# First channel tile's base beside the last projection tiles, and a new memory layout for the branches' stage

## What is computed

```
z = h @ in_w                                  # stage P: 92 tiles of 128 channels
r, k, v = mix(z_rkv, shift(z_rkv), mu)        # branch A: token shift on a 4-row grid, then a mix
kk = l2_normalize(k * k_k)                    # per head of 64
decay, a = lora(...)                          # per direction
y_A = sum over directions of the chunked RWKV recurrence (chunks of 128 tokens)
q, k, v = silu(conv3(z_qkv)); k, q = l2_normalize(k), l2_normalize(q)
y_B = sum over directions of the chunked gated delta rule (chunks of 128 tokens)
y = concat(groupnorm(y_A) ..., rmsnorm(y_B) ...)
```

## Time and profile before

| | us |
|---|---|
| median of 3 runs | 4016.66 (4015.81 to 4019.03) |
| profiled execution | 4017.41 |
| its span in the profile | 4015.6 |
| TensorE busy (matmul) | 3739.2 (93%) |
| VectorE, ACT, POOL busy | 2098.3 (52%), 1504.2 (37%), 1654.0 (41%) |
| stage P | 1300 to 2047 |
| stage B | 2047 to 3054 |
| stages C and M | 3063 to 4015 |

### The profile page before, as it was taken

The page is one execution under the profiler, slowest core; times in us unless marked ns, Lnnn a source line. Parts: engine busy times, 40 slices in busy tenths (PEclk is TensorE's granted clock), DMA queues, the critical chain, the costliest instruction groups (busy, mean ns, idle before and its releaser), DMA issues. The chain is left out here.

```text
span 4015.6 us, 86008 instructions
## 1 busy us (share of the span) xinstructions
PE 3739.2 (93%) x37240; PEld 3456.6 (86%) x37240; DVE 2098.3 (52%) x3807; ACT 1504.2 (37%) x2641; POOL 1654.0 (41%) x1192
## 2 busy tenths in 40 slices
PE   6998999898899899999979999999998999999998
PEld 5888888788888788888868888888887999999998
DVE  4434433533443677666766666666655653434343
ACT  3333343333343443232223333333333444444343
POOL 4444455444454454333321111111113656666664
PEclk9999999899999999999979999999998999999999
DMA  4344444344444576767720000001004545555553
GB/s 186 142 173 153 162 173 169 134 158 158 145 158 160 174 273 245 276 245 267 284 76 27 27 19 14 23 27 27 7 2 170 190 177 183 184 181 183 184 187 128
DMA packets 115672, 587.21 MB, mean 146 GB/s; under 512 B 20832, under 2 KB 40160, under 8 KB 50528
## 3 DMA queue, kind: packets, MB, share of 16 engines
q1 hardware_dynamic: 115296, 581.71, 40.8%
HBM read 560.95 MB, written 20.71 MB: 145 GB/s over the span
## 5 line engine op out<-in xcount | busy, mean ns | idle before, releaser
L543 PE MATMUL bank<-act_L,part_L 128*128 128x256 f32 x7296 | 972.2, 292 | 5.7 <-POOL act_L L3020 4.0
L543 PEld LDWEIGHTS bank<-act_L,part_L 128*128 128x128 f32 x7296 | 923.8, 197 | 46.4 <-issue 25.9
L2980 POOL TENSOR_TENSOR part_L<-wring,part_L 128x512 fp32r<-128x512 f32 x304 | 528.4, 1739 | 631.9 <-ACT part_L L1311 631.8
L543 PE MATMUL bank<-act_P,part_P 128*128 128x512 f32 (+1 forms) x3488 | 716.9, 365 | 18.1 <-POOL part_P L2980 12.7
L2980 POOL TENSOR_TENSOR part_C<-wring,part_C 128x512 fp32r<-128x512 f32 x320 | 568.7, 1786 | 369.9 <-ACT part_C L1311 369.9
L543 PEld LDWEIGHTS bank<-act_P,part_P 128*128 128x128 f32 x3488 | 591.3, 189 | 137.6 <-DVE arena_P L2408 16.2
L543 PE MATMUL bank<-arena_B 64*64 64x64 f32 (+4 forms) x13472 | 567.1, 227 | 28.7 <-DVE arena_B L2485 19.0
L543 PEld LDWEIGHTS bank<-arena_B 64*64 64x64 f32 (+3 forms) x13472 | 512.5, 141 | 70.2 <-DVE arena_B L2485 22.3
L2022 DVE TENSOR_TENSOR part_L<-wring,part_L 128x512 fp32r<-128x512 f32 x304 | 228.9, 754 | 524.8 <-ACT part_L L1311 524.8
L2980 POOL TENSOR_TENSOR part_P<-wring,part_P 128x512 fp32r<-128x512 f32 x184 | 307.0, 1674 | 432.0 <-ACT part_P L1311 432.0
L543 PE MATMUL bank<-act_Y,part_C 128*128 128x258 f32 (+1 forms) x3840 | 464.7, 283 | 9.3 <-POOL part_C L2980 9.3
(11 more groups left out here) (248 smaller groups left out, 3459.4 us busy)
## 6 DMA issues: line engine op xcount, KB each, us to landing
wring<-in_w SPq DMA_DIRECT2D x404, 1024.0 KB, 4.8
arena_P<-in_w SPq DMA_DIRECT2D x64, 1024.0 KB, 5.0
mring<-in_w SPq DMA_DIRECT2D x32, 1024.0 KB, 5.7
z_kept<-arena_P SPq DMA_DIRECT2D x34, 256.0 KB, 5.6
z_kept<-arena_P SPq DMA_DIRECT2D x58, 128.0 KB, 5.9
xT<-z_kept SPq DMA_DIRECT2D x26, 256.0 KB, 2.7
arena_C<-z_kept SPq DMA_DIRECT2D x32, 128.0 KB, 2.8
cst<-z_kept SPq DMA_DIRECT2D x24, 128.0 KB, 2.1
```

Source lines behind the costliest of these rows:

```text
L543: return e.matmul(out, lhsT, rhs, start=start, stop=stop)
L2980: e.tensor_tensor(wl[:, 4:8, :], wring[s % NS][:, 8 * j + 4:8 * j + 8, :], wh[:, 4:8, :].bitcast(F32), sub).then_inc(*mark("pool_lo", "lop ...
```

## The change

Three things are done together.

1. The memory of stage B gets names. The arena is cut into seven parts by what stage P has in them: `parts` (weights), `h` (activations, with `yr` in it), `made` (norm buffers, free after tile 16), `mid` (modulation), `stores` (the four buffers `B.zst`) and `top` (not used by stage P). What tile 0's base writes goes into `made` and `top`; what only the tails and the second direction's end use (`R.pr`, `R.bon`, `R.tp`, `R.s`, `R.bv`, `R.gate`, `g.Y`) goes into `stores`. So the wait of ACT, VectorE and POOL for the last four stores at the start of stage B is gone; VectorE waits for them just ahead of `R.pr` in the preparation of direction 0.
2. `base_a(0)` is taken out of stage B and runs in stage P's `early`, after tile 84; the loop `base_a` in stage B begins at tile 1. The word `("base", 0)` has then been said when stage B begins. `FIRST_B`, `PAD` and the `LATE` constants stay. The load of tile 0's LoRA weights moves to SP's `early`, behind `load_b(0)`.
3. The clearing for direction 0 is shared out anew: VectorE clears `NA` and `AK` ahead of everything in stage B (`rzv`), POOL clears `RK`, `RB`, `XT` right after direction 0's copies of the identity, and direction 1's copies move behind branch B's.

```diff
@@ -378,18 +378,23 @@
-            pools = [arena_(37088), xT_] + wring_ + [cst[:, o:o + 1920], par[:, PAR["wa2"][0]:PAR["wa2"][0] + 512]]
-            used = [0] * len(pools)
-
-            def alloc(n, order=(0, 1, 2, 3, 4, 5, 6)):
+            whole_B = arena_(37088)
+            pools = {"xT": xT_, "cst": cst[:, o:o + 1920], "wa2": par[:, PAR["wa2"][0]:PAR["wa2"][0] + 512]}
+            pools.update((f"w{i}", x) for i, x in enumerate(wring_))
+
+            pools.update((name, whole_B[:, a:b]) for name, a, b in (
+                ("parts", 0, 8192), ("yr", 8192, 12288), ("h", 12288, 24576), ("made", 24576, 26880), ("mid", 26880, 32000),
+                ("stores", 32000, 34048), ("top", 34048, 37088)))
+            used = dict.fromkeys(pools, 0)
+
+            def alloc(n, order=("parts", "h", "mid", "w0", "w1", "w2", "xT", "cst", "wa2", "top", "made", "stores")):
                 for i in order:
-                    whole = pools[i]
-                    if used[i] + n <= whole.shape[1] - (4096 if i == 0 else 0):
+                    if used[i] + n <= pools[i].shape[1]:
                         used[i] += n
-                        return whole[:, used[i] - n:used[i]]
+                        return pools[i][:, used[i] - n:used[i]]
                 raise MemoryError(n)
-            B.yr = pools[0][:, 37088 - 4096:].rearrange("p (k t) -> p k t", k=16)
-            early = (1, 5, 6)
+            B.yr = pools["yr"].rearrange("p (k t) -> p k t", k=16)
+            early = ("xT", "cst", "wa2")
@@ -400,6 +405,12 @@
+            R.kT, R.vT, R.kkn, R.z = [alloc(512, ("made",)) for _ in range(4)]
+            R.rT = alloc(256, ("made",))
+            lo_ = alloc(768, ("top",))
+            R.Vt = [alloc(512, order) for order in (("top",), ("parts",))]
+            R.rrk = alloc(256, ("top",))
+            R.pr, R.bon, R.tp, R.s, R.bv, R.gate = [alloc(256, ("stores",)) for _ in range(6)]
@@ -410,10 +421,9 @@
-            lo_ = alloc(768)
             R.lo = lo_.rearrange("p (j c) -> p j c", j=6)
-            R.kT, R.vT, R.z, R.a, R.cc, R.e1, R.e2, R.kkn = [alloc(512) for _ in range(8)]
-            R.Vt = [alloc(512).rearrange("p (q c) -> p q c", q=4) for _ in range(2)]
+            R.a, R.cc, R.e1, R.e2 = [alloc(512) for _ in range(4)]
+            R.Vt = [x.rearrange("p (q c) -> p q c", q=4) for x in R.Vt]
@@ -429,9 +439,8 @@
-            R.rT, R.rrk, R.pr, R.bon, R.tp, R.s, R.bv, R.gate = [alloc(256) for _ in range(8)]
             for g in R.d:
-                g.Y, g.Rd = alloc(256), alloc(256)
+                g.Y, g.Rd = alloc(256, ("stores",)), alloc(256)
@@ -937,6 +969,8 @@
+                yield from weave.until(("ptile", 84))
+                yield from base_a_tile(0)
@@ -1922,8 +1940,6 @@
-            for n in range(NPR - 4, NPR):
-                w.wait_ge(done("zs", n))
@@ -2409,6 +2425,40 @@
+
+            def base_a_tile(c):
+                V = "dve_rwkv"
+                yield
+                for key, dst, n in (("r", R.rT, c), ("k", R.kT, 8 + c)):
+                    w.wait_ge(done("z", key, c))
+                    w.wait_ge(done("part", key, c))
+                    stt(dst, D.S[key], P("mu", n, 1), dst, mult, add).then_inc(*mark(V, "mixed", key, c))
+                yield
+                w.wait_ge(done("z", "v", c))
+                w.wait_ge(done("part", "v", c))
+                w.wait_ge(done("mixed", "k", c))
+                ts(R.kkn, R.kT, P("kk", c, 1), None, mult, None).then_inc(*mark(V, "kk0", c))
+                ts(R.rrk, R.rT, P("rk", c, 1), None, mult, None).then_inc(*mark(V))
+                stt(R.vT, D.S["v"], P("mu", 16 + c, 1), R.vT, mult, add).then_inc(*mark(V, "mixed", "v", c))
+                yield
+                BS.take()
+                b, u = BS.take()
+                w.wait_ge(done("sums", ("kk", c)))
+                ts(small(2), b[:, 0:8], 1.0, 1e-12, mult, add).then_inc(*mark(V, "free", "bs", u))
+                counts.at[("mean", ("kk", c))] = counts.last(V)
+                yield
+                b, u = BS.take()
+                w.wait_ge(done("spread", ("kk", c)))
+                tt(R.kkn, R.kkn, b, mult).then_inc(*mark(V, "free", "bs", u))
+                counts.at[("zfree", c, 0)] = counts.last(V)
+                yield
+                weave.said.add(("base", c))
+
+            def base_a():
+                for c in range(1, 8):
+                    yield from weave.until(("prep", c - 1, 1))
+                    yield from weave.rest(LATE_A)
+                    yield from base_a_tile(c)
@@ -2547,6 +2599,8 @@
+                    for n in range(NPR - 4, NPR):
+                        w.wait_ge(done("zs", n))
@@ -2578,6 +2632,7 @@
+                    w.wait_ge(done("rzv"))
@@ -2622,41 +2677,6 @@
-            def base_a():
-                V = "dve_rwkv"
-                for c in range(8):
-                    if c:
-                        yield from weave.until(("prep", c - 1, 1))
-                        yield from weave.rest(LATE_A)
...
-                    if c == 0:
-                        for x in (R.d[0].NA, R.d[0].AK, R.d[0].RK, R.d[0].RB, R.d[0].XT):
-                            e.memset(x, 0.0).then_inc(*mark(V, "rz", 0))
...
@@ -2849,8 +2869,8 @@
-            for n in range(NPR - 4, NPR):
-                w.wait_ge(done("zs", n))
+            for x in (R.d[0].NA, R.d[0].AK):
+                e.memset(x, 0.0).then_inc(*mark("dve_rwkv", "rzv"))
@@ -3069,9 +3089,15 @@
+            def early():
+                yield from weave.until(("ptile", 84))
+                yield from base_a_tile(0)
+
             def tail(stage, n0, n1):
                 for n in range(n0, n1):
                     yield from project(stage, n)
+                    if stage == "P":
+                        weave.said.add(("ptile", n))
@@ -3203,18 +3231,19 @@
-            weave.run(tail("P", 0, NPR), behind=behind)
+            weave.run(tail("P", 0, NPR), early(), behind=behind)
             weave.run(behind)
             ends("pool", "P")
             begins(w, "P")
-            for n in range(NPR - 4, NPR):
-                w.wait_ge(done("zs", n))
-            for d in range(2):
-                for Q in R.d[d].Q:
-                    e.tensor_copy(Q.rearrange("p (u s) -> p u s", u=8), bc(C("id64"), 8)).then_inc(*mark("pool_rwkv", "qid", d))
+            for Q in R.d[0].Q:
+                e.tensor_copy(Q.rearrange("p (u s) -> p u s", u=8), bc(C("id64"), 8)).then_inc(*mark("pool_rwkv", "qid", 0))
+            for x in (R.d[0].RK, R.d[0].RB, R.d[0].XT):
+                e.memset(x, 0.0).then_inc(*mark("pool_rwkv", "rz", 0))
             for d in range(2):
                 for Q in G.d[d].Q:
                     e.tensor_copy(Q.rearrange("p (u s) -> p u s", u=4), bc(C("id64"), 4)).then_inc(*mark("pool_gdn", "gqid", d))
+            for Q in R.d[1].Q:
+                e.tensor_copy(Q.rearrange("p (u s) -> p u s", u=8), bc(C("id64"), 8)).then_inc(*mark("pool_rwkv", "qid", 1))
@@ -3368,6 +3397,7 @@
+                e.dma_start(lo_, LORA[0]).then_inc(*mark("dma_lora", "lora", 0))
@@ -3379,8 +3409,8 @@
-                w.wait_ge(done("gate", i - 1) if i else done("w0h"))
-                e.dma_start(lo_, LORA[i]).then_inc(*mark("dma_lora", "lora", i))
+                    w.wait_ge(done("gate", i - 1))
+                    e.dma_start(lo_, LORA[i]).then_inc(*mark("dma_lora", "lora", i))
```

More of the change, by code:

```diff
@@ L3087, in gpsimd, with base_a_tile, base_a @@
             ends("pool", "L")
+            def base_a_tile(c):
+                for _ in range(3):
+                    yield
+                root(("kk", c), small(2), 8)
+                yield
+                yield
+                weave.said.add(("base", c))
+            def base_a():
+                for c in range(1, 8):
+                    yield from weave.until(("prep", c - 1, 1))
+                    yield from weave.rest(LATE_A)
+                    yield from base_a_tile(c)
             def inverse(tag, XP, XT, Q, n, sem):
@@ L3123, in thread_a @@
                     weave.said.add(("chain", c, d))
-            def base_a():
-                for c in range(8):
-                    if c:
-                        yield from weave.until(("prep", c - 1, 1))
-                        yield from weave.rest(LATE_A)
-                    for _ in range(3):
-                        yield
-                    root(("kk", c), small(2), 8)
-                    yield
-                    yield
-                    weave.said.add(("base", c))
             def tail_a():
```

120 lines of the change are left out of this document (49 added, 71 removed).

## The result

The changed kernel takes 4077.53 us (median of 5 runs, 4074.4 to 4086.23) against 4019.03 us for the kernel before beside it (5 runs, 4015.81 to 4022.39): ratio 1.0148, 95% interval 1.0133 to 1.0163. The forecast was 4055.7 us in a range of 4004 to 4080, with 0.69 on slower. Side and mechanism hold; the size is 22 us short, more than a third of the loss. The profiled execution of the kernel after took 4086.23 us; it is the slowest of the five, 8.7 us above their median, and its mean granted clock is 0.961 where the other four have 0.963. So sizes read from it are some 9 us larger than the median's, and by that difference of 0.002 over 4080 us about 8 of the 9 belong to the clock (an estimate).

What follows compares the result with a forecast made beforehand. TensorE (93% busy) was taken to decide on the average, but what counts is whether VectorE is loaded in the same steps. 4017.4 - 6 (start) + 45 (phase) = 4056.4, less 0.75: 4055.7 us, range 4004 to 4080.

Steps and rivals of the forecast that it cites:

- The seam (part 1): Seam between projections and branches: direction 0 starts 13.8 - 2.7 = 11.1 us earlier, its transposes at 2063.0.
- The start (part 2): First period of stage B: the earlier start is worth 6 us, between 2 and 14.
- The phase (part 3): Stage B's periods: A six steps ahead of B makes VectorE's bursts meet, +6.4 us seven times, 45 us.
- The steps named: Sign in stage B: TensorE waits for VectorE where B's convolutions (L2764/L2766/L2772) stand beside A's preparation (L2561 to L2565).
- The other pair that was named: Sign in stage B: TensorE also waits for VectorE where L2716 stands beside L2547; no separate size.
- a step lasts as long as the longer of the two: Stage B: each step takes the longer of TensorE's and VectorE's work; 121.0 us a period before, 127.8 after.
- Rival (c): Stage B: low clock behind 14 new waits, 14 x 3 = 42 us more, 4098; chance 0.06 above 4080.
- one in three: Stage B: only one in three of the 14 new waits brings the low clock, 4070, inside the range.
- Rival (a): Stage B: phase costs nothing, bursts slip into VectorE's 38% free; 4010.7 us, from 4003 to 4015; chance 0.22.
- (b): Both halved: start -6, phase +1 to +2 us a period, seven times; 4018 to 4025; chance 0.10.
- (d): Seam: TensorE stalls beside the projection for the root, start gives 3 instead of 6 us; no chance of its own.
- The end of the stage: End of stage B: A finishes six steps earlier, B's last chain runs alone; 0 to +2 us, taken as 0.

Runs made afterwards that it cites:

- e4: Kernel after with FIRST_B = 5 instead of 10, branch A one step further ahead of B than in the kernel before: 4029.10 us, ratio 1.0030.
- e1: Kernel after with FIRST_B = 4 instead of 10, so both branches stand to each other as in the kernel before: 4006.92 us, ratio 0.9975.
- e3: Kernel after with tile 0's base put back behind the seam, keeping the new memory layout and moved loads: 4016.99 us, ratio 1.0000.
- e6: Kernel before without two of the three taps of each convolution of branch B: 4013.40 us, ratio 0.9989.
- e2: Kernel before with FIRST_B = 16 instead of 10, putting branch A six steps ahead of B: 4086.97 us, ratio 1.0174.
- e5: Kernel after without two of the three taps of each convolution of branch B: 4038.89 us, ratio 1.0051.
- e11: Kernel after with branch B's tanh of k on ScalarE issued one step later, behind branch A's copies: 4090.52 us, ratio 1.0180.
- e7: Kernel after with FIRST_B = 7 instead of 10, branch A three steps further ahead of B than in the kernel before: 4078.52 us, ratio 1.0151.
- e10: Kernel before with LATE_B = 7 instead of 3, branch B's base pieces four steps later: 4066.74 us, ratio 1.0123.
- e12: e1 with branch B's tanh of k on ScalarE issued one step later: 4008.37 us, ratio 0.9978.

## Why the prediction was right, and where it was short

**The seam (part 1)** held in its times: lw at "about 2051" came at 2051.09 and at full clock, the transposes expected at 2063.0 came at 2063.91, and the last projection matmul ended 2.3 us later, near the 2.7 priced for TensorE's added work. One pair of traces can't confirm that price, though: in the traces of kernels that are the same up to there, this matmul ends anywhere from 2048.11 (e4) to 2053.36 (e1) with the base beside the projection, and from 2046.83 (e3) to 2049.28 (e6) without. One of its grounds was wrong: the wait for the last stores, named first among what is removed, had held nothing up by itself, since e3, which removes it without moving the base, is at 1.0000.

**The start (part 2)** is the first wrong step. It was to be worth 6 us at the point where branch A's step 28 and branch B's step 22 end, at 2120 against 2126. They end at 2126.51: worth nothing. Its first stretch is right (put at 2080, measured 2078.76). The second, twelve steps, was priced at 27.9 us of work, 6.5 for the low clock and 6 of waiting, 40 us; it took 47.75, of which 9.9 are waiting and, with the 27.9 of work taken as they were priced, 9.9 the clock (10.3 by the low stretches of the trace). So the hole was not closed but moved: from the seam to this point TensorE is idle for 27.2 us, after 28.3 before. Up to the transposes the waits shrink from 18.78 us (7.36 + 3.22 + 8.20) to 12.54 (1.67 + 10.87), but behind them 14.6 follow, as I read it since branch A runs alone there at first and TensorE has nothing of branch B to put between. With branch B brought back beside it (e1), the stage is 10.4 us shorter than before: the start is worth more than the 6 us, but only with the phase kept.

**The phase (part 3)** is right in its mechanism. The steps named (L2764 and L2766 beside L2561 to L2565) are where the 3.2 us wait stands; e1 and e2 show that the shift is the cause, e5 and e6 that more than half of it is the convolutions on VectorE meeting branch A's preparation, and e11 that ScalarE's order in between is not. The rest, by the waits, is branch B's chain updates behind the same preparation. The other pair that was named, L2716 beside L2547, ends none of TensorE's waits in stage B of the kernel after. The periods were to be 126 to 128 us. Counted from lw of direction 1 in one tile to that in the next, the seven are 125.9 to 133.1, 129.3 in the mean, against 120.1 before. The term was put at +6.4 us a period and is +9.2 in the profiled run, and it is two terms: +4.2 of waiting (idle time of 6.9 us a period before, 11.0 after), which the sum over-priced by half, and 4.9 of clock (2.4 before, 7.3 after), which had no place in it; in the median run the clock's part is about 1 us smaller. So the step that failed is "a step lasts as long as the longer of the two": it is a rule for waits, somewhat high for them, and blind to what comes behind them. That the measured time still lies in the range, 2.5 us under its top, is partly luck: the waits were priced some 15 us too high and the clock's 28 to 37 us were left out, beside the 6 of the start.

**Rival (c)** had the missing term, and its price was right for the wrong number: 14 waits of 2 to 3 us at 3 us each, 42 us; measured are 37 us for the clock, on top of 30 instead of 45 us of waiting. Nor were there 14 waits of that size but seven, of 2.8 to 3.2 us; of the other new ones between 2130 and 2970 us none is over 1.4. It was given "one in three" inside the range and 0.06 above it. The trace of before had the warning, a window at 0.50 behind a wait of 1.18 us and 80 us of low clock in the stage; a change that adds waits of nearly three times that length in seven places must be priced with the clock in the sum, not beside it. The Trainium skill (TensorE: Matmul & The Clock Gate, "HAM oscillation") tells of waits that come again and again, there for DMA, and bring the clock down each time. The trace agrees in that the low clock came at each of the seven longest waits and fills 161 us of stage B instead of 80; how long it lasts is not the same each time here, 3.4 to 13.7 us.

**Rival (a)**, that the phase costs nothing because VectorE has 38% of its time free, is refuted. VectorE is busy only 491 of 840 us in the kernel after (526 before, when more of the work fell into them), and is nevertheless what the added time hangs on. The Trainium skill (Perfetto Trace Analysis, "Identifying the Most-Contended Engine") has the engine with the highest occupancy optimized first, for TensorE judged rather by its weight loads than by its matmuls. That is TensorE by either (85% and 92%). The trace does not bear that order out here: VectorE's 3.96 us a period weigh 38.6 us in one order of the steps and 4.0 in the other. (b) and (d) did not come about.

The end of the stage was taken at 0 to +2 us; stage C's first matmul was put at about 3100 and came at 3133.70, late by the missing term and the start, and nothing behind it changed.

## What to carry to other kernels

Where two streams are interleaved in fixed steps, add up each step's work per engine before anything is started earlier: a start that moves one stream against the other changes every later period, and seven periods outweigh any seam. The cure is then to move the other stream by the same amount (here FIRST_B = 4 instead of 10, which turns +58.5 us into -10.7). And when waits of a microsecond or more are added to a stream of matmuls, price the lower clock behind them at about as much as the waits themselves, in the sum and not beside it; that is the middle of a wide spread (see below), so the range must take it in too.

## What was not expected of the hardware

- A wait can cost more through the clock than by itself. Per us of added idle time, the clock took 1.2 us in the kernel after (37.0 for 30.0), 1.6 in e7 (47.5 for 28.9 against e1) and 4.7 in e10's profiled run (72.2 for 15.3), but 0.7 in e2 (26.9 for 38.4). In e12 3.8 us more of waiting than in e1 went with 8.1 us less for the clock. Part of this is the error of the split; why the rest differs so much was not settled.
- The same kernel can be given different clocks: e10's five runs lie from 4063.94 to 4097.98 us, with mean granted clocks of 0.962 and 0.951.
- One weave step of shift (e4) cost 22.2 us with only 8.7 us more waiting. Its clock column is 16.3 us higher. The busy shares hardly show it: TensorE's is 791.32 of 840 us in e4 and 795.01 in e1.
